# GpSimd takes over part of VectorE's work in the second block's attention

## What is computed

```
qa, kv  = parts of h @ w_in           # 8 query heads, 2 key/value heads, three branches of k and v
o_cmp   = attention over 31 compressed keys        (no rotation)
o_slc   = causal attention, rotated q and k        (selected blocks)
o_win   = causal attention, rotated q and k        (window)
o_a     = sigmoid gates weigh o_cmp, o_slc, o_win and add them
o_d     = banded attention of its own q, k, v, rotated, with a sink per head   ("local branch")
o_b, o_c = convolution and pooling branches of parts of h @ w_in
x      += norm((gates(h) * up(o_a, o_b, o_c, o_d)) @ w_o)      # then a feed-forward part
```

## Time and profile before

| | |
|---|---|
| median of three runs | 4252.24 us |
| profiled execution, its own time | 4252.23 us |
| profiled execution, span from first to last instruction | 4250.2 us |
| TensorE (PE) busy | 4071.5 us, 96% |
| VectorE (DVE) busy | 2008.9 us, 47% |
| GpSimd (POOL) busy | 1129.6 us, 27% |
| ScalarE (ACT) busy | 846.2 us, 20% |
| mean granted TensorE clock | 0.972 |

### The profile page before, as it was taken

How to read it: one execution, slowest core, us unless ns; L and a number is a source line. 1 busy time by engine, 2 the same in 40 slices (tenths; PEclk the granted TensorE clock), 3 DMA queues, 4 the chain that set the end, 5 groups by cost and what they waited for, 6 DMA issues and landing times. The chain is left out here.

```text
span 4250.2 us, 52350 instructions
## 1 busy us (share of the span) xinstructions
PE 4071.5 (96%) x19141; PEld 3037.2 (71%) x19141; DVE 2008.9 (47%) x3647; ACT 846.2 (20%) x1844; POOL 1129.6 (27%) x894
## 2 busy tenths in 40 slices
PE   7998999999999799999989999999999899999998
PEld 3446958887666488865578847888745688478887
DVE  2445544422342433223457625785334677247852
ACT  2332210001333211003330111111123401111110
POOL 0003414443000144420026300444300254004443
PEclk9998999999999799999999999999899999999999
DMA  6211224324341133253213231332441133322322
GB/s 226 71 48 35 79 61 123 109 86 122 110 137 33 45 89 89 84 121 65 51 45 90 80 89 50 89 89 84 95 91 38 48 90 89 83 56 79 89 84 74
DMA packets 622411, 352.27 MB, mean 83 GB/s; under 512 B 68714, under 2 KB 592267, under 8 KB 622260
## 3 DMA queue, kind: packets, MB, share of 16 engines
q1 hardware_dynamic: 607368, 327.46, 28.8%
q10 hardware_dynamic: 14892, 22.78, 1.6%
HBM read 340.22 MB, written 2.62 MB: 81 GB/s over the span
## 5 line engine op out<-in xcount | busy, mean ns | idle before, releaser
L810 PE MATMUL psum<-h_normed,weight_slot 128*128 128x256 f32 x2688 | 612.0, 381 | 2.0 <-ACT h_normed L498 1.7
L810 PEld LDWEIGHTS psum<-h_normed,weight_slot 128*128 128x128 f32 x2688 | 513.5, 191 | 74.6 <-issue 4.1
L735 POOL TENSOR_TENSOR weight_slot<-weight_slot 128x512 f32<-128x512 f32 (+1 forms) x132 | 177.4, 1344 | 876.2 <-DMA weight_slot<-in_w_ffn_in 286.1
L902 DVE COPY work<-psum 128x256 f32<-128x256 f32 x100 | 42.1, 421 | 595.0 <-PE psum L810 595.0
L3030 PE MATMUL psum<-sums_of_h,weight_slot 128*128 128x256 f32 x1280 | 282.8, 379 | 0.0
L3030 PEld LDWEIGHTS psum<-sums_of_h,weight_slot 128*128 128x128 f32 x1280 | 243.6, 190 | 32.7
L2624 PE MATMUL psum<-h_normed,weight_slot 128*128 128x512 f32 x576 | 255.4, 602 | 1.0 <-ACT raw L2807 1.0
L810 PE MATMUL psum<-sums_in,weight_slot 128*128 128x256 f32 x1056 | 242.5, 380 | 2.4 <-DVE sums_in L847 2.4
L810 PE MATMUL psum<-sums_hidden,weight_slot 128*128 128x256 f32 x1056 | 243.7, 380 | 0.0
L1320 PE MATMUL psum<-h_normed,weight_slot 128*128 128x512 f32 x512 | 225.1, 594 | 1.6 <-PEq L202 1.6
L810 PE MATMUL psum<-sums_of_h,weight_slot 128*128 128x256 f32 x960 | 220.5, 380 | 3.5 <-POOL weight_slot L741 3.5
(11 more groups left out here) (515 smaller groups left out, 6531.4 us busy)
## 6 DMA issues: line engine op xcount, KB each, us to landing
weight_slot<-in_w_ffn_in SPq DMA_DIRECT2D x88, 512.0 KB
weight_slot<-in_ffn_w_up SPq DMA_DIRECT2D x88, 512.0 KB
weight_slot<-in_w_gate SPq DMA_DIRECT2D x64, 512.0 KB
weight_slot<-in_w_in SPq DMA_DIRECT2D x40, 512.0 KB, 5.5
weight_slot<-in_dsw_w_in SPq DMA_DIRECT2D x36, 512.0 KB, 7.0
weight_slot<-in_gdn_w_in SPq DMA_DIRECT2D x32, 512.0 KB, 15.2
weight_slot<-in_w_ffn_out SPq DMA_DIRECT2D x64, 256.0 KB
tile_ahead<-in_w_ada SPq DMA_DIRECT2D x16, 1024.0 KB, 7.5
```

The source lines that it names most:

```text
L735: nc.gpsimd.tensor_tensor(b(self.S1), b(self.A21), b(self.A22), ALU.add).then_inc(self.folded, 1)
L810: last = nc.tensor.matmul(c.ps[:, 4 * bank + r // 2, (r % 2) * self.HALF:(r % 2 + 1) * self.HALF], c.slots[s][:, b * 512 + k * P:b * 512 + ...
L902: nc.vector.tensor_copy(u4, p(self.P1)).then_inc(self.link, 1)
```

## The change

Three pieces of work go from VectorE to GpSimd.

- The rotations of KD, QD0 and QD1 (`FAR` = 3 of seven). GpSimd does the multiplication by sin and the addition right behind its multiplication by cos, each waiting for the one before; semaphores `crossed_far` and `rotated_far`. `cross` is now indexed by `i % 2`.
- The four differences of h, in group 1, on GpSimd behind the last rotation and ahead of `ahead.fold`.
- In local rounds head `a` = 1 is scaled by GpSimd, one `tensor_scalar` for each of two tiles, after VectorE's reciprocal; `weighed_far`. VectorE scales only `a` = 0. TensorE's transposes wait for both.

A bank has 54 semaphores in place of 52.

```diff
@@ gpsimd, in each group
                 for i, t in enumerate(ROPED):
                     n = g * 7 + i
                     pool.wait_ge(copied, g * NT + (t + 1))
-                    if n >= 2:
-                        pool.wait_ge(rotated, n - 1)
-                    nc.gpsimd.tensor_tensor(cross[:, n % 2, :], raw[:, t, :], rope[:, 0, :], ALU.mult).then_inc(turned_with_cos, 1)
-            ahead.fold(pool, 0)
+                    if 2 <= i < 6:
+                        pool.wait_ge(rotated, g * NEAR + (i - 1))
+                    elif n >= 2:
+                        pool.wait_ge(rotated_far, g * FAR + (i >= NEAR))
+                    nc.gpsimd.tensor_tensor(cross[:, i % 2, :], raw[:, t, :], rope[:, 0, :], ALU.mult).then_inc(turned_with_cos, 1)
+                    if i >= NEAR:
+                        pool.wait_ge(swap_landed[i % 3], landed(g, i))
+                        nc.gpsimd.tensor_tensor(roped[:, i, :], roped[:, i, :], rope[:, 1, :], ALU.mult).then_inc(crossed_far, 1)
+                        pool.wait_ge(crossed_far, g * FAR + (i - NEAR + 1))
+                        pool.wait_ge(turned_with_cos, n + 1)
+                        nc.gpsimd.tensor_tensor(roped[:, i, :], roped[:, i, :], cross[:, i % 2, :], ALU.add).then_inc(rotated_far, 1)
+                if g == GROUPS - 1:
+                    for n in range(4):
+                        ahead.sum_inputs(pool, nc.gpsimd, n)
+                    ahead.fold(pool, 0)
+                for u in range(NSA_ROUNDS, NR):
+                    w, tiles = rounds[u]
+                    pool.wait_ge(inverse_ready, g * NR + (u + 1))
+                    for i in range(len(tiles)):
+                        p = probs[:, u % RING, 1, i * w:(i + 1) * w]
+                        ins = nc.gpsimd.tensor_scalar(p, p, stats[:, 2, u % RING, 1, i:i + 1], None, ALU.mult)
+                    ins.then_inc(weighed_far, 1)
@@ tensor
                         if t == NSA_ROUNDS:
-                            pe.wait_ge(rotated, g * 7 + 7)
+                            pe.wait_ge(rotated_far, g * FAR + FAR)
...
                         pe.wait_ge(weighed, g * NR + (u + 1))
+                        if u >= NSA_ROUNDS:
+                            pe.wait_ge(weighed_far, g * NSWA + (u - NSA_ROUNDS + 1))
@@ vector
-                for i in range(4):
+                for i in range(NEAR):
                     rotate(i)
...
                 for t in range(NR + 1):
-                    if t in (1, 4, 5):
-                        rotate({1: 4, 4: 5, 5: 6}[t])
-                    if g == GROUPS - 1 and t in (7, 9, 11, 13):
-                        ahead.sum_inputs(dve, (t - 7) // 2)
...
-                        for a in range(2):
+                        for a in range(2 if br != SWA else 1):
@@ SevenSteps
-    def sum_inputs(self, dve, n):
+    def sum_inputs(self, engine, ops, n):
...
         if n in (1, 3):
-            dve.wait_ge(self.t_in, (n + 1) // 2)
+            engine.wait_ge(self.t_in, (n + 1) // 2)
         to, a, b = of[n]
-        nc.vector.tensor_tensor(to, a, b, ALU.subtract).then_inc(self.t_in, 1)
+        ops.tensor_tensor(to, a, b, ALU.subtract).then_inc(self.t_in, 1)
```

More of the change, by code:

```diff
@@ L58 @@
 SLOT = 4096
-BANK = 52
+BANK = 54
 def bucket_of(dist):
@@ L2508, in attend, with landed @@
     assert all(w * len(tiles) <= S for w, tiles in rounds)
+    NEAR, FAR = 4, 3
+    def landed(g, i):
+        in_group, before = sum(1 for x in range(NEAR + FAR) if x % 3 == i % 3), i // 3 + 1
+        return 16 * 4 * (g * in_group + before)
     def first_key_tile(br, qt):
@@ L2529, in attend @@
         norm = Norm(c, sems[39:43], None, layer_gain(c, "norm_mix_pre_2", layer), bank=NORM_BANK)
-        kc_loaded, compress_loaded, gates_done, squashed, gates_turned, gates_ready, gate_w_loaded = sems[43:50]
+        kc_loaded, compress_loaded, gates_done, squashed, gates_turned, gates_ready, gate_w_loaded, rotated_far, weighed_far, crossed_far = sems[43:53]
         gate_rows = raw[0:24, QD0, :]
@@ L2704, in _ @@
                         if t == 2:
-                            pe.wait_ge(rotated, g * 7 + 4)
+                            pe.wait_ge(rotated, g * NEAR + NEAR)
                             pe.wait_ge(v_ready, g * 2 + 2)
                         if t == NSA_ROUNDS:
-                            pe.wait_ge(rotated, g * 7 + 7)
+                            pe.wait_ge(rotated_far, g * FAR + FAR)
                         pe.wait_ge(turned_copied, g * NR + (t + 1))
@@ L2891, in rotate @@
                 def rotate(i):
-                    sem = swap_landed[i % 3]
-                    of_group, before = sum(1 for x in range(7) if x % 3 == i % 3), i // 3 + 1
-                    dve.wait_ge(sem, g * (SWAP * of_group) + SWAP * before)
+                    dve.wait_ge(swap_landed[i % 3], landed(g, i))
                     nc.vector.tensor_tensor(roped[:, i, :], roped[:, i, :], rope[:, 1, :], ALU.mult).then_inc(crossed, 1)
-                    dve.wait_ge(crossed, g * 7 + (i + 1))
+                    dve.wait_ge(crossed, g * NEAR + (i + 1))
                     dve.wait_ge(turned_with_cos, g * 7 + (i + 1))
-                    nc.vector.tensor_tensor(roped[:, i, :], roped[:, i, :], cross[:, (g * 7 + i) % 2, :], ALU.add).then_inc(rotated, 1)
-                for i in range(4):
+                    nc.vector.tensor_tensor(roped[:, i, :], roped[:, i, :], cross[:, i % 2, :], ALU.add).then_inc(rotated, 1)
+                for i in range(NEAR):
                     rotate(i)
```

## The result

The changed kernel takes 4283.36 us (median of 4 runs, 4280.86 to 4286.09) beside 4252.31 us for the kernel before (4 runs): ratio 1.0077, 95% interval 1.0065 to 1.0089. It is slower by some 31 us; forecast were 4281 us, in a range of 4260 to 4288.

The account below looks back on a forecast made before the run. The prediction took TensorE, busy 96% of a 4250.2 us span, to bound the kernel, so only its stalls mattered. Two layers of 3.8 (first group) plus 10.9 (second group), local rounds 0, added 29.4 to 4252.23: 4281 us, range 4260 to 4288.

Parts of the forecast that it names:

- The rule that prices the change: Beside busy GpSimd, each VectorE scaling with both ends in SBUF costs one GpSimd operation, 1.34 us for 512 columns.
- Prices: GpSimd two-input operations: 256 columns 0.759 us, 512 columns 1.26, each sum of 1024 columns an estimated 2.3 us.
- First group, rotations: Second block's attention, first group: GpSimd's rotation operations stall round 2's scalings, moving the mask of round 5 by +3.8 us.
- Within half a us of the same shift: Layer 1's first group: the mask of round 5 ends within half a us of layer 0's +3.8 us shift.
- Second group: Rotations, sums and fold stall scalings of rounds 1 and 2: round 5's mask +13.0, moved sums gain 2.1, net +10.9 us.
- Local rounds: Rounds 13 to 15, scalings split between engines: taken as 0, bounds over four groups -6.8 to +4.5 us.
- the upper bound, 0.759: Local rounds: GpSimd's 256-column scaling priced at the nearest two-input row, 0.759 us each, giving +1.1.
- The sum: Both layers: 2 x (3.8 + 10.9) = 29.4 us on 4252.23 us, giving 4281 us.
- narrow scalings pass in pairs: Rival, rounds 1 and 2: two narrow scalings pass in each GpSimd gap; 4260 us, chance 0.15 for all narrow ones.
- they don't contend: Rival, second group's round 1: 31-wide scalings run free of GpSimd; +6.7 us there, 4273 us; 0.20 shared with 31s in pairs.
- the work is free: Rival, rounds 1 to 5 of the second group: GpSimd's work costs nothing, 10 us faster, 4242 us; chance 0.07.
- Dear local scalings: Rival, local rounds: GpSimd's scalings are dear, at their upper bound, 4286 us; chance 0.06.

Follow-up runs that it names:

- the gap alone: Kernel before with VectorE's four sums of h moved between the two groups, fold operations left where they were: 4250.67 us, ratio 0.9997.
- the gap with the gates: Kernel before with VectorE's four sums between the groups and each GpSimd fold operation waiting for the scaling of round 7, 8, 9 or 10: 4243.03 us.
- the third kernel: Changed kernel with all seven rotations on VectorE again, GpSimd's sums following its last cosine product: 4261.67 us, ratio 1.0023.

## Why the prediction was right, step by step

- *The rule that prices the change* (one GpSimd operation to each scaling) held where GpSimd's two-input operations follow one another: seen in the rows of after, and shown by the split sums, the moved sums and the merged scaling. It is narrower than the prediction put it: the reciprocal didn't wait, and in the local rounds a scaling didn't wait for a whole GpSimd scaling (below). The passage of the Trainium skill named in the prediction (SBUF — State Buffer, Who interferes with whom) agrees; the question that it left open, who is next, this case answers for operations that follow with no more than 0.1 us between them: GpSimd's next one, nearly always.
- *Prices*: the sums took 2.34 us, estimate 2.3. (Half of what the Trainium skill gives for 2048 columns in GPSIMD Engine Reference, Elementwise — side-by-side cycle accounting, is 2.25: 4% too short here.)
- *First group, rotations*: forecast +3.8 at mask(5), measured +3.4 in layer 0 and +4.7 in layer 1. From mask(5) to mask(13) it had nothing, and there lie another 1.0 and 1.5 us: after its wait TensorE came back to 2.4 GHz later. Timeline of PE, then tables of windows, after and before (PEclk is the third number from the right):

```profile
2000.32 1.97 PE L2766 MATMUL psum<-ident,probs 128*128 128x128 f32 x8 [4.91 <-DVE probs L2976]
...
2007.60 1.98 PE L2794 MATMUL psum<-probs_t,v_rows 128*64 128x128 f32 x16
```

```profile
2000.00:2010.00 10.00, 9.68 (x52) 7.11 (x54) 6.41 (x16) 5.00 (x14) 0.00 (x0) 0.50 0.01 2
```

```profile
2000.00:2010.00 10.00, 9.82 (x78) 7.03 (x80) 7.97 (x20) 6.55 (x18) 0.00 (x0) 0.74 0.00 0
```

  The granted clock was 0.50 (1.2 GHz) in these 10 us, and 0.74 on the mean before; there TensorE went into the transposes without a wait, and the same first product of 16 took 1.09 us, at 2005.22. The stall alone doesn't decide this. In layer 0 of the kernels with the sums taken back and with the sums moved, TensorE was at 1.2 GHz already ahead of its wait (round 1's transposes took 1.92 and 1.91 us, in the changed kernel 1.06), the wait was 3.38 us in place of 4.91, and mask(5) to mask(13) took 24.5 us, as before the change; in the eight other groups with this stall it took 25.2 to 25.6. What decides it stays open.

  "Within half a us of the same shift" for layer 1 was too small: 6.2 us in place of 3.8. But one pair of traces is a thin base for this. Eight first groups of layers 0 and 1 have nothing changed up to mask(13) (the kernel before, only the local halves, the gap alone, the gap with the gates): they took 38.4 to 40.5 us from mask(2) to mask(13), the two of the kernel before 40.48 and 38.42. Ten have the far rotations on GpSimd and eight separate scalings: 43.9 to 45.1 us. The means lie 5.1 us apart, 4.1 up to mask(5) and 1.0 behind it. So a first group cost some 5.1 us in place of 3.8, and the difference of 4.4 and 6.2 is mostly that of the two groups before.
- *Second group*: mask(3) +4.1 (forecast +4.4, with `cmpmul` at 1.23 us paying the fourth operation), mask(5) +12.4 (+13.0), the sums' removal from rounds 7 to 13 -2.1 (-2.1): +10.4 against +10.9; in layer 1 +10.9.
- *Local rounds*: the total was right at 0, by terms that were not. GpSimd's scaling of 256 columns was taken at 0.4 us and took 0.99:

```profile
2041.67 1.98 POOL L2624 TENSOR_SCALAR probs<-probs,stats 128x256 f32<-128x256 f32 x2 [2.44 <-DVE stats L2966]
```

  It even lies above the upper bound, 0.759. Yet most of its time is hidden: the next mask runs on VectorE meanwhile, and the distance of the masks of rounds 15 and 16 fell from 4.26 to 3.96 us, that of rounds 14 and 15 from 4.01 to 3.74. The end loses more than that: TensorE's transposes of round 15 begin 5.39 us after mask(16), 4.41 before. By these rows a group would be 0.4 us longer; the kernel with the local halves alone doesn't show it (-0.7 us, not to be told from 0). Nor did the scalings take turns by whole operations. Timeline of DVE:

```profile
2041.61 0.84 DVE L2972 TENSOR_SCALAR probs<-probs,stats 128x256 f32<-128x256 f32 x2
```

  VectorE's two are over at 2042.45, while GpSimd's first runs from 2041.67 to 2042.75; VectorE's second took 0.57 us, its first 0.35. So it waited some 0.2 us and not for a whole GpSimd operation. Why stays open.
- *The sum*: 2 x (3.8 + 10.9) = 29.4 against 31.8 in the rounds. The mis-sized term is the first group's: 10.6 for two layers in this pair of traces (10.2 by the means above), not 7.6.
- *Rivals.* That narrow scalings pass in pairs is refuted for those of 128 columns (13.90 us for eight). For those of 31 the changed kernel shows the full price (five before GpSimd's operation of 2124.97, three with an operation each, `cmpmul` with the fourth), the kernel with the rotations taken back a part of it (six operations for eight). That they don't contend is refuted by the same rows. That the work is free falls by the time. Dear local scalings: dear they were, but hidden.
- *Not foreseen*: an edit's price depends on the others. Rotations on GpSimd push its sums past round 1, from scalings of 31 columns to those of 128; taking them away doesn't remove all collisions, it moves them.

## What to carry to other kernels

Before moving work from VectorE to an idle GpSimd, count the VectorE operations on SBUF that will run beside it, scalings and those with two SBUF inputs above all, and multiply by the length of one GpSimd operation: many narrow ones in a row are the dearest company. The product is an upper bound: in the local rounds, where GpSimd's operations are few, VectorE lost 0.2 us and not a whole operation. GpSimd's work is free where VectorE idles or works on PSUM; a semaphore wait can put it there, operation by operation. Where they must meet, merge VectorE's operations and keep GpSimd's short.

## What the runs showed of the hardware that was not expected

- GpSimd waits too: a sum of 2.34 us took 3.21 us when it met VectorE's product of 1024 columns (itself 3.33 us beside GpSimd, 1.22 alone).
- A GpSimd scaling by a number per partition took 0.99 us for 256 columns; one of 496 columns in the next stage took 0.605. The price goes by more than columns.
- Between two sums in the third kernel lies a gap of 0.08 us. One scaling of 31 columns (0.22 us alone) passed at such a gap, and one between two operations of `fold`; the other six each waited for a GpSimd operation to end.
- Not every VectorE operation on SBUF waits: the reciprocal of 8 columns kept its 0.19 us inside a GpSimd sum, in both layers.
